# A hybrid decoder trunk on one core: the feed-forward layer in two phases, with seven products per 2x2 block in both

## The chip, the cores and the metric

The kernel runs on one core of one Trainium2 chip. The metric is the device time of one execution in microseconds (us), as the median of three runs.

## What is computed

One step of a decoder layer on 512 new prompt positions (with 16 learned positions ahead of them) and 32 sampled positions, all float32, with a model width of 2048. Attention, a short convolution and a matrix memory are merged by an output projection; then comes the feed-forward layer, which is all that this change touches:

```
x = layer_norm(ALPHA * x + h @ w_out, ln1_g, ln1_b)
u = jax.nn.relu(x @ w_up)                       # w_up 2048 x 8192
return layer_norm(ALPHA * x + (u * u) @ w_down, ln2_g, ln2_b)   # w_down 8192 x 2048
```

It works on 544 columns, one for each position that is an output.

## The kernel before, in words

`phase_project`, `phase_mix`, `phase_out` and `phase_ff` follow one another. `phase_ff` (from L1996) is written out by hand for each engine; semaphores alone order the engines against each other.

**Three matmuls per product.** Every float32 operand is split into a high part, rounded to the type fp32r, and a low part, the difference. ScalarE writes the high part of a weight piece (`high`, L2271), VectorE subtracts it (`low`, L2385), and `third` (L2144 to L2146) makes high x high, high x low and low x high. The parts of the weights lie in rings of three slots, `ring_h` and `ring_l`, each slot 128 x 1024 (8 tiles of 128 x 128). The names `wh`, `big_wh`, `wl`, `big_wl` in a profile are those slots; `big_G` is the PSUM (eight banks); `raw` holds four pieces of raw weights; `base` is a large buffer with `y`, the residual sum in 16 tiles of 128 x 544, and the features `u2` behind it.

**Blocks.** The 8192 features go in 32 blocks of 256 (two tiles of 128). For one block, `up` makes its features from `x`. This product is laid out as 2x2: two feature tiles by two halves of the model width, times two halves of the width by two halves of the columns (272 each). Seven products stand in for eight (Winograd's form of Strassen's scheme): VectorE makes four sums of the weights (`combine`, L2401), the matching sums of `x` were made once, and the results are put together by copies on ScalarE (`copy`, L2311) and additions on VectorE (`accumulate`, L2404). An up block has 7 products x 8 tiles x 3 = 168 matmuls of 128 x 272.

**Down at once.** The features are cut at zero and squared (`relu_square`, L2388), split (`u_high` L2280, `u_low` L2392), and `down` multiplies them with the two row tiles of `w_down` in the ordinary way: 16 output tiles x 2 halves x 2 x 3 = 192 matmuls of 128 x 272. Each output tile is added to `y` by `add` (L2398), so `y` is read and written once per block.

The order is up 1 (plain), down 0, then thirty times up of block b+1 and down of block b (`ff_block` on each engine), then `down_last`, which makes the last down product with the columns as rows and the second layer norm. SyncE (SP) loads the weights: `load_up` (L2090), 512 KB in rows of 512 B, and `load_down` (L2094), 512 KB in rows of 2 KB. GpSimd (POOL) has no work in `phase_ff` until its end.

## Time and profile before

| | us |
|---|---|
| three runs | 2879.74, 2884.47, 2887.08 |
| median | 2884.47 |
| span of the profiled execution | 2886.8 |
| PE busy | 2790.1 (97%) |
| VectorE busy | 1930.4 (67%) |
| ScalarE busy | 889.8 (31%) |
| GpSimd busy | 213.1 (7%) |
| DMA, mean over the span | 196 GB/s |

The profiled execution's own time isn't listed apart; its span, from the first to the last instruction, is 0.3 us under the longest of the three runs. PE is TensorE, PEld its weight loads, DVE VectorE, ACT ScalarE. Matmul records overlap one another in time, so how many of them start in a stretch says more than their durations.

### The profile page before, as it was taken

The page shows a single profiled execution, that of the slowest core. Times are in us where ns is not written, and L with a number is a line of the kernel's source. Part 1 is how long each engine was busy: PE and PEld are TensorE (multiplying, and loading weights), DVE is VectorE, ACT ScalarE, POOL GpSimd, SP SyncE. Part 2 cuts the span into 40 slices and gives each one's busy share as a digit, 9 for nine tenths or more (in the row PEclk, how much of TensorE's full clock was granted, in tenths as well). Part 3 has the DMA queues.
Part 4 walks back from the last instruction along what each step waited for, and adds up shares of the span by engine and source line. Part 5 has one row for each costly group of instructions (what it writes and reads, how often), then busy time and mean ns, then how long its engine had stood idle before and what let it go on. Part 6 is the DMA issues. An engine that isn't in the chain of part 4 may idle for free.

```text
span 2886.8 us, 59355 instructions
## 1 busy us (share of the span) xinstructions
PE 2790.1 (97%) x25779; PEld 2644.1 (92%) x25779; DVE 1930.4 (67%) x2358; ACT 889.8 (31%) x1343; POOL 213.1 (7%) x242
## 2 busy tenths in 40 slices
PE   8999999999999888999999999999999999999997
PEld 8988988888888666999899999999999999999996
DVE  3374555555454586888877777777777777777776
ACT  3221222122122355445523223232232323223232
POOL 3010101101110221111000000000000000000002
PEclk9999999999999899999999999999999999999999
DMA  7889999999999823677323232332323323233232
GB/s 242 307 317 383 412 386 414 409 400 407 396 409 353 282 77 96 172 208 203 92 74 111 67 115 88 88 110 67 117 74 103 103 74 115 66 113 91 86 110 106
DMA packets 379733, 565.95 MB, mean 196 GB/s; under 512 B 22219, under 2 KB 287020, under 8 KB 369058
## 3 DMA queue, kind: packets, MB, share of 16 engines
q1 hardware_dynamic: 302562, 351.68, 37.0%
q0 software_dynamic: 13872, 141.28, 12.1%
q10 hardware_dynamic: 63040, 69.21, 7.0%
q8 instruction: 203, 3.33, 0.5%
q14 instruction: 56, 0.46, 0.0%
HBM read 526.26 MB, written 35.84 MB: 195 GB/s over the span
## 4 chain that ended last, share of the span: by engine, by line
PE 49%; DVE 2%; ACT 0%; DMA 0%; issue 0%; ACTq 0%
PE big_G L2144 16%; PE big_G L2146 16%; PE big_G L2145 16%; DVE ff_mv L2551 0%; DVE ff_out L2556 0%; DVE wl L2385 0%; DMA raw<-in_w_down 0%; PE big_G L2236 0%; DVE base L2401 0%; ACT ff_out L2361 0%; DVE ff_stats L2538 0%; DVE ff_out L2593 0%; ACT wh L2271 0%; DVE base L2398 0%; PE big_G L2232 0%
## 5 line engine op out<-in xcount | busy, mean ns | idle before, releaser
L2398 DVE SCALAR_TENSOR_TENSOR base<-big_G,base 128x544 f32<-128x544 f32 x496 | 358.3, 722 | 230.8 <-PE big_G L2146 230.6
L469 PE MATMUL prj_G<-prj_xh,prj_wh 128*128 128x280 f32 (+1 forms) x1696 | 501.8, 296 | 5.2 <-ACT prj_stage L609 3.3
L471 PE MATMUL prj_G<-prj_xh,prj_wl 128*128 128x280 f32 (+1 forms) x1696 | 496.2, 293 | 0.0
L470 PE MATMUL prj_G<-prj_xl,prj_wh 128*128 128x280 f32 (+1 forms) x1696 | 495.2, 292 | 0.0
L724 DVE STREAM_TRANSPOSE prj_kT<-base 128x4096 f32<-128x4096 f32 x64 | 284.5, 4445 | 263.4 <-PE prj_S L502 260.4
L2271 ACT ACTIVATE wh<-raw 128x1024 fp32r<-128x1024 f32 x227 | 239.4, 1059 | 652.9 <-PE big_G L2146 534.9
L2144 PE MATMUL big_G<-ff_uh,wh 128*128 128x272 f32 x1328 | 382.2, 288 | 1.9 <-DVE base L2398 1.9
L2145 PE MATMUL big_G<-ff_ul,wh 128*128 128x272 f32 x1328 | 383.4, 289 | 0.0
L2146 PE MATMUL big_G<-ff_uh,wl 128*128 128x272 f32 x1328 | 383.4, 289 | 0.0
L469 PEld LDWEIGHTS prj_G<-prj_xh,prj_wh 128*128 128x128 f32 x1696 | 322.4, 190 | 30.0 <-issue 29.3
L2385 DVE TENSOR_TENSOR wl<-raw,wh 128x1024 fp32r<-128x1024 f32 x227 | 277.1, 1221 | 82.0 <-ACT wh L2271 82.0
L471 PEld LDWEIGHTS prj_G<-prj_xh,prj_wl 128*128 128x128 f32 x1696 | 322.4, 190 | 0.0
L470 PEld LDWEIGHTS prj_G<-prj_xl,prj_wh 128*128 128x128 f32 x1696 | 322.2, 190 | 0.0
L2144 PEld LDWEIGHTS big_G<-ff_uh,wh 128*128 128x128 f32 x1328 | 249.4, 188 | 2.4 <-DVE base L2398 2.3
L707 DVE TENSOR_TENSOR prj_wl<-prj_raw,prj_wh 128x1024 fp32r<-128x1024 f32 x106 | 127.1, 1210 | 184.6 <-ACT prj_wh L579 182.9
L2145 PEld LDWEIGHTS big_G<-ff_ul,wh 128*128 128x128 f32 x1328 | 250.3, 188 | 0.0
L2146 PEld LDWEIGHTS big_G<-ff_uh,wl 128*128 128x128 f32 x1328 | 249.7, 188 | 0.0
L2271 ACT ACTIVATE big_wh<-raw 128x1024 fp32r<-128x1024 f32 x113 | 119.6, 1059 | 325.9 <-PE big_G L2146 260.7
L579 ACT ACTIVATE prj_wh<-prj_raw 128x1024 fp32r<-128x1024 f32 x106 | 111.4, 1057 | 339.1 <-DMA prj_raw<-in_w_in 266.5
L2144 PE MATMUL big_G<-big_xh,wh 128*128 128x272 f32 x688 | 201.2, 292 | 1.7 <-ACT base L2274 1.7
L2146 PE MATMUL big_G<-big_xh,wl 128*128 128x272 f32 x688 | 199.2, 289 | 0.0
L2145 PE MATMUL big_G<-big_xl,wh 128*128 128x272 f32 x688 | 197.8, 288 | 0.0
(463 smaller groups left out, 6239.2 us busy)
## 6 DMA issues: line engine op xcount, KB each, us to landing
prj_v_nat<-in_cache_v SPq DMA_DIRECT2D x242, 512.0 KB, 8.4
raw<-in_w_up SPq DMA_DIRECT2D x128, 512.0 KB, 4.5
raw<-in_w_down SPq DMA_DIRECT2D x128, 512.0 KB, 4.5
prj_raw<-in_w_in ACTq DMA_DIRECT2D x103, 512.0 KB
raw<-in_w_out SPq DMA_DIRECT2D x60, 512.0 KB, 4.7
prj_scratch<-prj_stage ACTq DMA_DIRECT2D x53, 280.0 KB, 9.8
out_xr<-x_scratch SPq DMA_DIRECT2D x32, 272.0 KB, 5.3
base<-in_cache_v SPq DMA_DIRECT2D x14, 512.0 KB, 7.9
```

Of the source, the lines that this page charges most:

```text
L469: mm(out, w_hi[:, k, m], xh[:, k0 + k, cols], start=(first and k == 0), stop=False)
L470: mm(out, w_hi[:, k, m], xl[:, k0 + k, cols], start=False, stop=False)
L471: last = mm(out, w_lo[:, k, m], xh[:, k0 + k, cols], start=False, stop=(end and k == nk - 1))
L579: A(wh[n % WH][:, :, :], raw[n % RAW][:, :, :], ACT.Copy).then_inc(hi_done, 1)
L707: V.tensor_tensor(wl[n % WH][:, :, :], raw[n % RAW][:, :, :], wh[n % WH][:, :, :].bitcast(F32), ALU.subtract).then_inc(lo_done, 1)
L724: V.transpose(flat(kT[:, :, :, :, :].rearrange("p r h b i -> p r (h b i)")), flat(k_nat[k % 2][:, :, :]))\
L2144: mm(out, w_hi, x_hi, start=start, stop=False)
L2145: mm(out, w_hi, x_lo, start=False, stop=False)
L2146: return mm(out, w_lo, x_hi, start=False, stop=stop)
L2271: A(ring_h[slot % RING], Q[q], ACT.Copy).then_inc(hi_done, 1)
L2385: V.tensor_tensor(ring_l[slot % RING], Q[q], ring_h[slot % RING].bitcast(F32), ALU.subtract).then_inc(lo_done, 1)
L2398: V.scalar_tensor_tensor(out, G[2 + t % 2][:, :, 0:HALF_M], 1.0 / ALPHA, out, ALU.mult, ALU.add).then_inc(y_done, 1)
```

## The change

The feed-forward layer no longer interleaves up and down products.

Phase one (`for g in range(NUP)`) makes the thirty up blocks 2 to 31, as seven products each. ScalarE now cuts and squares the features (`square`, two instructions of 128 x 1088). For blocks 1 to 30, GpSimd makes four sums of the block's quarters (`made_sum`), so that seven combinations of 128 x 272 lie side by side; ScalarE and VectorE split all seven at once (128 x 1904), and SP spills both parts to DRAM (`u_scratch`). They pass through the room of `y`, which is written to DRAM first (`y_scratch`) and read back at the end of the phase. Blocks 0 and 31 keep their old treatment.

Phase two (`for v in range(NVISIT)`) makes the down products of blocks 1 to 30. Six blocks form a chunk; five chunks by eight pairs of output tiles make 40 visits. A visit is a 2x2 product again, of two tile rows per block by two output tiles, with seven products of 6 tiles x 3 = 126 matmuls of 128 x 272. The combinations of a chunk stand in a window of 20 slots of 128 x 1632 (835,584 bytes each; 14 for a chunk, 6 for the beginning of the next), which takes the room that the split `x` had in phase one. Weight pieces are now 128 x 768 (393,216 bytes), in rows of 512 B, and five of them fit in `raw`.

In both phases one set of four PSUM banks belongs to even groups and one to odd ones, and some products are added onto a bank that already holds one (`onto`). A few semaphores of `phase_project` are cleared and freed, to have enough of them.

Cut to what is spoken of below (the old `ff_block` of each engine stands in the listing above):

```diff
+CH = 6
+NBLK = DFF // (2 * P)
+NUP = NBLK - 2
+NCHK = NUP // CH
+NPAIR = KT // 2
...
+            def fill_window(chunk, n, j):
+                at = 2 * COMBOS * chunk + 2 * n + j
+                slot = AT_SLOT[at % NSLOTS]
+                if at < NSLOTS:
+                    before = BEFORE[at][1]
+                    if before == 7:
+                        sp.wait_ge(combo_lo, NUP)
+                        sp.wait_ge(up_done, product_at(NUP - 1, 2))
+                    else:
+                        sp.wait_ge(up_done, product_at(NUP - 1, before))
+                else:
+                    was, m = divmod(at - NSLOTS, 2 * COMBOS)
+                    sp.wait_ge(up_done, product_at(NUP + NPAIR * was + NPAIR - 1, m // 2))
+                sp.dma_start(window[:, slot, :, :].bitcast(F32), dram["u_scratch"][chunk, j, PLACE[n]]).then_inc(win_in[n], 16)
...
+            for g in range(NUP - 1):
+                sp.wait_ge(lo_done, base_of(g) + 5)
+                load_role(g + 1, 0)
+                sp.wait_ge(sum_done, sums_of(g) + 4)
+                load_role(g + 1, 3)
+                sp.wait_ge(lo_done, base_of(g) + 6)
+                load_role(g + 1, 2)
+                sp.wait_ge(lo_done, base_of(g) + 7)
+                load_role(g + 1, 1)
+                spill(g + 1)
+            g = NUP - 1
+            refill_y(0)
+            for m in range(3):
+                fill_window(0, m // 2, m % 2)
+            sp.wait_ge(lo_done, base_of(g) + 5)
+            load_role(g + 1, 0)
+            for m in range(3, 5):
+                fill_window(0, m // 2, m % 2)
+            sp.wait_ge(lo_done, base_of(g) + 6)
+            load_role(g + 1, 2)
+            sp.wait_ge(lo_done, base_of(g) + 7)
+            load_role(g + 1, 1)
+            load_role(g + 1, 3)
+            for m in range(5, 8):
+                fill_window(0, m // 2, m % 2)
+            spill(g + 1)
+            for m in range(8, 14):
+                fill_window(0, m // 2, m % 2)
+            refill_y(1)
...
+                    for j in range(2):
+                        fill_window(chunk + 1, 3, j)
+                    for j in range(2):
+                        fill_window(chunk + 1, 4, j)
+                    load_next(g, 1)
+                    for j in range(2):
+                        fill_window(chunk + 1, 5, j)
+                    load_next(g, 2)
+                    for j in range(2):
+                        fill_window(chunk + 1, 6, j)
+                    load_next(g, 3)
...
+                    elif wide and n in (3, 5, 6):
+                        pe.wait_ge(copied, 4 + 4 * g + {3: 1, 5: 3, 6: 4}[n])
+                    elif n in (3, 5, 6):
+                        pe.wait_ge(y_done, y_adds(v) + {3: 1, 5: 4, 6: 5}[n])
...
+            def square(b):
+                ac.wait_ge(added, 3 * (b - 1))
+                A(whole_u(b), whole_u(b), ACT.Relu).then_inc(positive, 1)
+                ac.wait_ge(positive, b - 1)
+                A(whole_u(b), whole_u(b), ACT.Square).then_inc(relu_done, 1)
+            def combos_high(b):
+                i = half_of(b)
+                ac.wait_ge(sums_made, 4 * b)
+                if b <= 2:
+                    ac.wait_ge(y_out, 16)
+                else:
+                    ac.wait_ge(spilled[i], 32 * ((b - 1) // 2))
+                A(split[i][0].bitcast(F32R), combos(b), ACT.Copy).then_inc(combo_hi, 1)
+            for n in range(3):
+                high_of(0, n)
+            for g in range(NUP):
+                b, banks = block_of(g), banks_of(g)
+                high_of(g, 3)
+                if b > 2:
+                    ac.wait_ge(combo_lo, b - 2)
+                copy(block_u(b, 0, 0), banks[0], g, 0)
+                high_of(g, 4)
+                if g > 0:
+                    square(b - 1)
+                high_of(g, 5)
+                copy(block_u(b, 1, 0), banks[3], g, 2)
+                copy(block_u(b, 0, 1), banks[0], g, 3)
+                high_of(g, 6)
+                combos_high(b - 1)
+                copy(block_u(b, 1, 1), banks[2], g, 4)
+                for n in range(3):
+                    next_high(g, n)
...
+            def third_and_second(g):
+                low_of(g, 2)
+                dv.wait_ge(*weights_in(g, 2))
+                combine(weights_of(g, 2), weights_of(g, 0), weights_of(g, 2), ALU.subtract)
+                dv.wait_ge(sum_done, sums_of(g) + 1)
+                dv.wait_ge(lo_done, base_of(g) + 3)
+                combine(weights_of(g, 3), weights_of(g, 3), weights_of(g, 2), ALU.subtract)
+            def first_sum(g):
+                dv.wait_ge(sum_done, sums_of(g) + 2)
+                combine(weights_of(g, 0), weights_of(g, 0), weights_of(g, 3), ALU.add)
+            def fourth_sum(g):
+                combine(weights_of(g, 1), weights_of(g, 1), weights_of(g, 3), ALU.subtract)
...
+            def last_add(g):
+                dv.wait_ge(up_done, product_at(g, 6))
+                dv.wait_ge(copied, 4 + 4 * g + 3)
+                accumulate(block_u(block_of(g), 0, 1), banks_of(g)[2])
+            for g in range(NUP):
+                b, banks = block_of(g), banks_of(g)
+                if g > 0:
+                    last_add(g - 1)
+                third_and_second(g)
+                low_of(g, 3)
+                dv.wait_ge(up_done, product_at(g, 1))
+                dv.wait_ge(copied, 4 + 4 * g + 1)
+                accumulate(block_u(b, 0, 0), banks[1])
+                first_sum(g)
+                low_of(g, 4)
+                fourth_sum(g)
+                low_of(g, 5)
+                low_of(g, 6)
+                dv.wait_ge(combo_hi, b - 1)
+                V.tensor_tensor(split[half_of(b - 1)][1].bitcast(F32R), combos(b - 1), split[half_of(b - 1)][0], ALU.subtract).then_inc(combo_lo, 1)
+                next_low(g, 0)
+                dv.wait_ge(up_done, product_at(g, 5))
+                dv.wait_ge(copied, 4 + 4 * g + 4)
+                accumulate(second_tile(b), twice(banks[0]))
+                next_low(g, 1)
...
+                third_and_second(g)
+                if v < NPAIR:
+                    dv.wait_ge(y_in[0 if p < 3 else 1], 16)
+                dv.wait_ge(up_done, product_at(g, 0))
+                to_y(y[:, left, HALVES[0]], banks[0])
+                low_of(g, 3)
+                dv.wait_ge(up_done, product_at(g, 1))
+                dv.wait_ge(y_done, y_adds(v) + 1)
+                to_y(y[:, left, HALVES[0]], banks[1])
+                first_sum(g)
+                dv.wait_ge(up_done, product_at(g, 2))
+                to_y(y[:, right, HALVES[0]], banks[3])
+                low_of(g, 4)
+                fourth_sum(g)
+                dv.wait_ge(up_done, product_at(g, 3))
+                to_y(y[:, left, HALVES[1]], banks[0])
+                low_of(g, 5)
+                low_of(g, 6)
+                dv.wait_ge(up_done, product_at(g, 4))
+                to_y(y[:, right, HALVES[1]], banks[2])
+                if v == NVISIT - NPAIR + 1:
+                    dv.wait_ge(combo_hi, LAST_BLK)
+                    V.tensor_tensor(ul_end, u2_end, uh_end.bitcast(F32), ALU.subtract).then_inc(combo_lo, 1)
+                next_low(g, 0)
+                dv.wait_ge(up_done, product_at(g, 5))
+                dv.wait_ge(y_done, y_adds(v) + 5)
+                to_y(two(y[:, right, :]), twice(banks[0]))
+                next_low(g, 1)
...
+            for b in range(1, NUP + 1):
+                po.wait_ge(relu_done, b + 1)
+                if b == 1:
+                    po.wait_ge(y_out, 16)
+                elif b > 2:
+                    po.wait_ge(combo_lo, b - 2)
+                made_sum(sum_of(b, "T3"), block_u(b, 1, 1), block_u(b, 0, 1), ALU.subtract)
+                made_sum(sum_of(b, "T1"), block_u(b, 0, 1), block_u(b, 0, 0), ALU.subtract)
+                po.wait_ge(sums_made, 4 * b - 3)
+                made_sum(sum_of(b, "T2"), sum_of(b, "T3"), block_u(b, 0, 0), ALU.add)
+                po.wait_ge(sums_made, 4 * b - 1)
+                made_sum(sum_of(b, "T4"), block_u(b, 1, 0), sum_of(b, "T2"), ALU.subtract)
```

**ScalarE, one block.** Before, from the features' split to the next block's first down weights (in names, `base<-big_G` is a copy of a result, 128x1024 a weight piece):

```order
L2280 ACTIVATE ff_uh<-base 128x1088 [waits ff_down_ps,ff_relu_done]
L2271 ACTIVATE wh<-raw 128x1024 [waits ff_sum_done,ff_up_done]
L2311 ACTIVATE base<-big_G 128x272 [waits ff_up_done,ff_low_done]
L2271 ACTIVATE wh<-raw 128x1024 [waits ff_sum_done,ff_up_done]
L2271 ACTIVATE big_wh<-raw 128x1024 [waits ff_up_done]
L2311 ACTIVATE base<-big_G 128x272 [waits ff_up_done]
L2271 ACTIVATE wh<-raw 128x1024 [waits ff_sum_done,ff_up_done]
L2311 ACTIVATE base<-big_G 128x272 [waits ff_up_done]
L2271 ACTIVATE wh<-raw 128x1024 [waits ff_up_done,ff_raw_full0]
L2271 ACTIVATE big_wh<-raw 128x1024 [waits ff_up_done,ff_raw_full2]
L2271 ACTIVATE wh<-raw 128x1024 [waits ff_up_done,ff_raw_full1]
```

After, group g of phase one. The names with prj_ are semaphores of `phase_project` whose numbers were given out anew: `prj_v_last1` is `up_done`, `prj_v_last0` is `lo_done`, `prj_att_in` is `hi_done`; `ff_made` is one of the two buffers of features:

```order
L2494 ACTIVATE wh<-raw 128x1024 [waits prj_v_last1,ff_sum_done]
L2540 ACTIVATE ff_made_20539<-big_G 128x272 [waits prj_v_last1,ff_combo_lo]
L2494 ACTIVATE big_wh<-raw 128x1024 [waits prj_v_last1,ff_sum_done]
L2553 ACTIVATE base<-base 128x1088 [waits ff_added]
L2555 ACTIVATE base<-base 128x1088 [waits ff_positive]
L2494 ACTIVATE wh<-raw 128x1024 [waits prj_v_last1,ff_sum_done]
L2540 ACTIVATE ff_made_20539<-big_G 128x272 [waits prj_v_last1] x2
L2494 ACTIVATE wh<-raw 128x1024 [waits prj_v_last1,ff_sum_done]
L2565 ACTIVATE base<-base 128x1904 [waits prj_aT_ps,ff_sums_made]
L2540 ACTIVATE ff_made_20539<-big_G 128x272 [waits prj_v_last1]
L2494 ACTIVATE big_wh<-raw 128x1024 [waits prj_v_last1,prj_small_in]
L2494 ACTIVATE wh<-raw 128x1024 [waits prj_v_last1,prj_pages_in]
L2494 ACTIVATE wh<-raw 128x1024 [waits prj_v_last1,prj_kt_done]
```

The last copy of a result now stands behind the split of the seven combinations, which waits for GpSimd (`ff_sums_made`); relu and square stand between the weight pieces of products 4 and 5.

**SP, end of phase one.** From the first part of `y` to the first weight piece of the second visit:

```order
L2244 DMA base<-y_scratch 128x6x544 [waits prj_aT_ps,ff_y_out]
L2237 DMA ff_window<-u_scratch 128x1632 [waits prj_v_last1] x3
L2211 DMA raw<-in_w_down 128x6x128 [waits prj_v_last0]
L2237 DMA ff_window<-u_scratch 128x1632 [waits prj_v_last1] x2
L2211 DMA raw<-in_w_down 128x6x128 [waits prj_v_last0] x2
L2211 DMA raw<-in_w_down 128x6x128
L2237 DMA ff_window<-u_scratch 128x1632 [waits prj_v_last1] x3
L2220 DMA u_scratch<-base 128x7x272 [waits ff_combo_lo]
L2220 DMA u_scratch<-base 128x7x272
L2237 DMA ff_window<-u_scratch 128x1632 [waits prj_v_last1,ff_combo_lo] x2
L2237 DMA ff_window<-u_scratch 128x1632 [waits prj_v_last1] x4
L2244 DMA base<-y_scratch 128x10x544 [waits prj_aT_done,ff_y_out]
L2211 DMA raw<-in_w_down 128x6x128 [waits ff_sum_done]
```

Fourteen fills, the last spill and both parts of `y` stand on this queue among the weights of the first visit and ahead of the first piece of the second.

**SP, last visit of a chunk.** From a fill for the next chunk in the visit before it:

```order
L2237 DMA ff_window<-u_scratch 128x1632 [waits prj_v_last1]
L2211 DMA raw<-in_w_down 128x6x128 [waits prj_v_last0]
L2237 DMA ff_window<-u_scratch 128x1632 [waits prj_v_last1] x4
L2211 DMA raw<-in_w_down 128x6x128 [waits prj_v_last0]
L2237 DMA ff_window<-u_scratch 128x1632 [waits prj_v_last1] x2
L2211 DMA raw<-in_w_down 128x6x128 [waits ff_sum_done]
L2237 DMA ff_window<-u_scratch 128x1632 [waits prj_v_last1] x2
```

Eight fills stand between the weight pieces that the next visit needs; all other visits have one or none.

## Rows read from the trace of the kernel before

**Rows 1.** The page: busy time of the engines and the granted clock in 40 slices.
```profile
PE 2790.1 (97%) x25779; PEld 2644.1 (92%) x25779; DVE 1930.4 (67%) x2358; ACT 889.8 (31%) x1343; POOL 213.1 (7%) x242
...
PE   8999999999999888999999999999999999999997
...
PEclk9999999999999899999999999999999999999999
```

**Rows 2.** The page: the chain of work that ended last.
```profile
PE 49%; DVE 2%; ACT 0%; DMA 0%; issue 0%; ACTq 0%
PE big_G L2144 16%; PE big_G L2146 16%; PE big_G L2145 16%; DVE ff_mv L2551 0%; DVE ff_out L2556 0%; DVE wl L2385 0%; DMA raw<-in_w_down 0%; PE big_G L2236 0%; DVE base L2401 0%; ACT ff_out L2361 0%; DVE ff_stats L2538 0%; DVE ff_out L2593 0%; ACT wh L2271 0%; DVE base L2398 0%; PE big_G L2232 0%
```

**Rows 3.** Busy time by stretch; columns as in its first line.
```profile
core 0: us, PE busy (x) PEld busy (x) DVE busy (x) ACT busy (x) POOL busy (x), PEclk, DMA share, GB/s
...
1900.00:2000.00 100.00, 100.00 (x793) 99.71 (x792) 74.14 (x87) 28.72 (x32) 0.00 (x0) 1.00 0.33 95
2000.00:2100.00 100.00, 100.00 (x793) 99.71 (x792) 74.07 (x87) 27.80 (x31) 0.00 (x0) 1.00 0.29 85
```

**Rows 4.** Waits of PE from 1409 to 2831 us: total, times, longest.
```profile
PE big_G L2144 <- DVE base L2398: 5.0, 4, 2.0
PE big_G L2144 <- ACT base L2274: 1.7, 1, 1.7
```

**Rows 5.** Groups by line and form, VectorE, 1409 to 2830 us: busy, mean ns.
```profile
L2398 DVE SCALAR_TENSOR_TENSOR base<-big_G,base 128x544 f32<-128x544 f32 x495 | 357.6, 722 | 230.1 <-PE big_G L2146 229.8
L2385 DVE TENSOR_TENSOR wl<-raw,wh 128x1024 fp32r<-128x1024 f32 x226 | 275.9, 1221 | 82.0 <-ACT wh L2271 82.0
L2401 DVE TENSOR_TENSOR raw<-raw 128x1024 f32<-128x1024 f32 x120 | 146.4, 1220 | 1.0
...
L2404 DVE TENSOR_TENSOR base<-base,big_G 128x272 f32<-128x272 f32 x120 | 52.1, 434 | 1.4
...
L2392 DVE TENSOR_TENSOR ff_ul<-base,ff_uh 128x1088 fp32r<-128x1088 f32 x31 | 39.9, 1286 | 0.5 <-ACT ff_uh L2280 0.5
```

**Rows 6.** The same for ScalarE.
```profile
L2271 ACT ACTIVATE wh<-raw 128x1024 fp32r<-128x1024 f32 x226 | 238.3, 1059 | 647.9 <-PE big_G L2146 529.9 <-DVE raw L2401 98.9 <-DMA raw<-in_w_down 18.9
...
L2280 ACT ACTIVATE ff_uh<-base 128x1088 fp32r<-128x1088 f32 x31 | 34.0, 1097 | 0.0
L2311 ACT ACTIVATE base<-big_G 128x272 f32<-128x272 f32 x90 | 34.0, 378 | 0.0
```

**Rows 7.** Timeline of VectorE in one block: start, duration, instruction, idle before.
```profile
2012.60 1.28 DVE L2392 TENSOR_TENSOR ff_ul<-base,ff_uh 128x1088 fp32r<-128x1088 f32 x1
2013.81 2.48 DVE L2401 TENSOR_TENSOR raw<-raw 128x1024 f32<-128x1024 f32 x2
2017.47 1.22 DVE L2385 TENSOR_TENSOR big_wl<-raw,big_wh 128x1024 fp32r<-128x1024 f32 x1 [1.19 <-ACT big_wh L2271]
2018.61 1.22 DVE L2401 TENSOR_TENSOR raw<-raw 128x1024 f32<-128x1024 f32 x1
2021.02 1.23 DVE L2385 TENSOR_TENSOR wl<-raw,wh 128x1024 fp32r<-128x1024 f32 x1 [1.19 <-ACT wh L2271]
```

**Rows 8.** Timeline where GpSimd and VectorE meet, both reading SBUF.
```profile
1355.99 1.22 DVE L1871 TENSOR_TENSOR big_wl<-raw,big_wh 128x1024 fp32r<-128x1024 f32 x1
1356.15 1.69 POOL L1698 TENSOR_TENSOR out_total<-out_total,base 128x272 f32<-128x272 f32 x1 [6.30 <-DVE base L1889]
1357.13 1.80 DVE L1871 TENSOR_TENSOR out_fourth_l<-raw,out_fourth_h 128x1024 fp32r<-128x1024 f32 x1
```

**Rows 9.** GpSimd line 1698: duration ns minimum, median, maximum.
```profile
L1698 POOL TENSOR_TENSOR out_total<-out_total,base x28: 767/962/1688, 1186.6 to 1374.7; 128x272 f32<-128x272 f32 x28
```

**Rows 10.** DMA traffic: GB/s in 40 slices of 2028 to 2044 us.
```profile
GB/s 36 82 236 266 225 312 399 394 404 344 344 348 326 293 293 288 293 265 92 0 59 83 202 305 334 286 42 41 0 0 0 0 0 0 0 56 77 184 307 348
...
raw<-in_w_up SPq DMA_DIRECT2D x4, 512.0 KB, 4.7
```

**Rows 11.** Busy time by stretch, in the cache stage; last column GB/s.
```profile
600.00:700.00 100.00, 98.12 (x1300) 87.77 (x1300) 53.50 (x30) 22.03 (x39) 11.22 (x8) 1.00 1.02 401
```

**Rows 12.** Busy time by stretch around a gap of PE.
```profile
190.00:194.00 4.00, 4.00 (x61) 3.84 (x64) 2.60 (x3) 2.54 (x8) 0.94 (x1) 1.00 0.79 277
194.00:198.00 4.00, 0.94 (x36) 0.68 (x27) 3.79 (x8) 0.00 (x0) 0.00 (x0) 1.00 0.94 378
198.00:202.00 4.00, 3.09 (x18) 3.10 (x19) 4.00 (x2) 1.54 (x2) 0.00 (x0) 0.75 0.63 237
202.00:206.00 4.00, 4.00 (x28) 4.00 (x27) 2.31 (x2) 0.00 (x0) 1.65 (x1) 0.82 0.22 45
```

563 lines of the change are left out of this document (322 added, 241 removed).

## The prediction

> **What bounds the kernel now.** I read the page first. TensorE is busy for 97% of the span and its clock is full nearly everywhere [rows 1]. The chain that ended last runs through three lines of `phase_ff`, the three matmuls of a product, for 48% of the span [rows 2]. Matmul records overlap, so I count starts: a stretch of 100 us in the feed-forward holds 793 matmuls, which makes 100 / 793 = 0.126 us for one of 128 x 272, with PE never idle, VectorE busy 74% and ScalarE 28% [rows 3]. In the whole layer PE waits 6.7 us [rows 4]. So this layer is worth its number of matmuls, and fewer of them are a gain as long as nothing else becomes the pace. The rest of the argument is about that.
>
> **What goes.** Before, the thirty down blocks have 30 x 192 = 5760 matmuls. Now 40 visits have 126 each, 5040. The up products stay at 30 x 168, and blocks 0 and 31 are as they were. 720 matmuls x 0.126 us = **-91 us**. A group of phase one takes 168 x 0.126 = 21.2 us of PE at the least, a visit 15.9 us.
>
> **Phase one.** The old block lasted 45.4 us (360 matmuls), and the work around the up products could spread under the down products. Now it must fit into 21.2 us. VectorE has per group eleven operations of 128 x 1024 at 1.14 from start to start [rows 7], three additions (two at 0.43, one of 544 columns at about 0.7 [rows 5]) and the low part of the seven combinations. The last is 128 x 1904, which no row shows. The step from 272 to 1088 columns costs 1.286 - 0.434 us for 816 columns, about 1.04 ns a column [rows 5], so it takes 1.29 + 816 x 0.00104 = 2.1 us. That is 16.2 of 21.2 us, so the sum fits. The order doesn't. Follow what must come one after the other, from `square` in one group to `square` in the next:
> - relu and square of 128 x 1088 on ScalarE, 2 x 1.10 [rows 6]: 2.2
> - GpSimd's four sums. One takes 0.77 alone [rows 9]. Where VectorE reads two operands of SBUF at the same time, the record grows to 1.69, since GpSimd starts when VectorE's instruction is over, and VectorE's next one takes 1.80 instead of 1.22 [rows 8]. Low parts 5 and 6 are then on VectorE, so I take two sums of each kind: 4.9
> - the high part of 128 x 1904, by ScalarE's step of (1.097 - 0.378) / 816 = 0.88 ns a column [rows 6]: 1.8
> - its low part: 2.1
> - on VectorE, in program order, next weights 0, second tile, next weights 1, last addition, weights 2, two sums of weights: five at 1.14 (the last, on its predecessor's result, 1.26 [rows 7]), 0.64 and 0.36: 6.8
> - high part 3, low part 3, an addition, a sum, high part 4: two trips to ScalarE of 1.2 [rows 7], then 1.14, 0.36 and 1.22: 5.1
>
> Together 22.9, with the remaining hand-overs 23.0 us. It is longer than PE's 21.2, so the group takes 23.0. PE will be seen to wait before product 7, whose bank is cleared by ScalarE's last copy, and this copy is queued behind the high part of the combinations. 30 x 1.8 = **+54 us**. Bounds: zero stall if the sums never meet VectorE (the loop is then 21.1), and 30 x 3.7 = +111 if all four do (6.8 in place of 4.9).
>
> The Trainium skill (SBUF — State Buffer, Who interferes with whom) says that a VectorE instruction with two SBUF inputs and a GpSimd instruction that reads SBUF hold the shared port for their whole length, and the other blocks. The trace agrees (1.69 and 1.80 above). By the rule alone, with VectorE always there first, the upper bound would be the forecast.
>
> **Between the phases.** All goes through SP's queue, in order. Rates: 512 KB pieces in rows of 512 B move at about 290 GB/s in a burst [rows 10], pieces with long rows at 401 [rows 11], so a fill is 0.836 MB / 401 = 2.1 us and a weight piece 0.393 MB / 290 = 1.4 us. Spills and `y` have rows of 1.1 and 2.2 KB; I take 350 and 400 GB/s for them, between these. From the end of the last but one spill there are queued: `y` part one 4.2, fourteen fills 29, five weight pieces 6.8 (the fifth is the second visit's first), the last spill 5.6, `y` part two 7.0: 52.7 us. That spill is done some 8.5 us into the last up group, so the piece lands at about 8.5 + 52.7 + 1.2 = 62.4 and is split by 64.2, where PE alone would want it at 23.0 + 15.9 = 39. So 25 us of waiting in the first visit and before the second, and about 2 for the clock: **+27 us**. The bounds are +12 (all at 400 GB/s or more) and +45.
>
> On the clock: a gap of some 3 us of PE was followed by 8 us at 0.75 and 0.82 [rows 12], which is 1.0 + 0.7 = 1.7 us lost. I add this to each wait of over 3 us.
>
> **Chunk changes.** In the last visit of a chunk, eight fills stand among the next visit's pieces. From product 1's end (2.3 us, and 1.3 until data flow) the queue has 8 x 2.1 + 3 x 1.4 = 21 us, so role 3, which product 3 of the next visit needs, lands at about 25.8 and is split (0.83 and 0.95 by the rates above) by 27.6. PE alone wants it at 15.9 + 4.5 = 20.4. 7.2 + 1.7 of clock = 8.9, four times: **+35 us**, bounds +16 and +56. In other visits a fill and four pieces are 7.7 of 15.9 us and hidden. The Trainium skill (DMA: Bandwidth & Descriptors, Specifications) gives 512 B as the size from which the full rate is reached. The rows differ (290 against 401 GB/s); by the rule the change of a chunk would cost 4 x 1.2 = 5 us less.
>
> **Visits otherwise.** VectorE has eleven operations of 128 x 768 (0.95, by the step above; 0.88 from start to start), six additions of 0.36 and one of 0.64, 12.5 of 15.9 us. The additions to `y` are one round per chunk instead of per block, 358 us of VectorE before [rows 5], but that cost nothing, being hidden. The tightest place is weights 4: product 2's addition, a sum, a trip to ScalarE and the low part end about 0.3 us before PE wants them. I take 0 and bound it by +0.6 a visit, 24 us. The first group waits for the copy of `y` to DRAM (4.5 MB, about 11 us, and the sums behind it): **+4 us**, bounds 0 and 10. The semaphore clearing and the end of the kernel: 0; the last products keep their form, and their loads are behind waits that end in the last visit.
>
> **Sum** against the profiled span: 2886.8 - 91 + 54 + 27 + 35 + 4 = 2915.8. The median of the runs lies 2.3 us under that span, so I forecast **2914 us**, 1.0% slower. The saving is real, but the work around it is late by more.
>
> **Rivals.**
> - *PE stays the pace in phase one.* GpSimd's sums fall into VectorE's waits (after low part 6 it has nothing to do until the combinations come), the loop closes in 21.2 us. For it: the loop is over by only 8%, and VectorE's sum is 76%. Against it: lows 5 and 6 lie where GpSimd starts. 2914 - 54 = 2860. With the queues also at their better bounds 2860 - 15 - 19 = 2826.
> - *All four sums collide.* 30 x 3.7 instead of 30 x 1.8: 2914 + 57 = 2971. This is what the rule on the shared port gives at its worst. Against it: VectorE has no work for most of that time.
> - *VectorE paces the visits.* 2914 + 24 = 2938. For it: 0.3 us of slack in a chain of eight operations.
> - *Some of each,* with a sum within 0.3% of before. 0.3%, 8.7 us, is about what a measurement here can tell from no change.
> - *The change doesn't do what it says.* The order of PE's queue has exactly 720 matmuls fewer; I give it nothing.
>
> **How the numbers follow.** My forecast (2890 to 2935) 0.49; visits paced by VectorE 0.12; all sums collide 0.07; these are slower: 0.68. PE stays the pace 0.20, faster. Within 0.3%: 0.12. The range is to hold 8 in 10: below, it takes in the first rival, and above, the third and a part of the second: 2855 to 2950.
>
> **What would show it.** Right, if a group of phase one takes about 23 us, with PE waiting 1 to 2 us for a copy of ScalarE's thirty times; if GpSimd's sums have records of 0.8 and 1.7 us side by side; if there are about 25 us of waiting around the first visit, for DMA; and four waits of 6 to 8 us at the third product of a chunk's first visit. Wrong in the main term, if the groups take 21.2 us, or if the visits take more than 16 us in a row.

## The result, and the profile after

The changed kernel takes **2947.2 us** (median of 4 runs, 2934.1 to 2965.0) against 2885.0 before (2879.7 to 2887.1): ratio 1.022, 95% interval 1.019 to 1.025. The forecast was 2914, range 2855 to 2950. The sign was right, the time lies just inside the range, and the change (+62 us) is twice the forecast one (+29). The profiled execution took 2945.5 us, its span is 2943.5.

The page of the changed kernel, to be read against [rows 1] and [rows 2]:

```profile
PE 2730.8 (93%) x25059; PEld 2566.0 (87%) x25059; DVE 1954.3 (66%) x2358; ACT 1086.4 (37%) x1593; POOL 357.2 (12%) x362
...
PE   8999999999998988999999999999969898989897
...
PEclk9999999999999999999999999999989999999998
...
DVE 16%; PE 15%; DMA 8%; ACT 7%; issue 3%; POOL 3%; SPq 0%; ACTq 0%; POOLq 0%
```

PE has its 720 matmuls fewer, and its share fell from 97% to 93%. The chain no longer rests on PE but passes from engine to engine. Waits of PE in three stretches, phase one, between the phases, and the visits after the first (total, times, longest), against 6.7 us in the whole layer before [rows 4]:

```profile
PE big_G L2356 <- ACT ff_made L2540: 19.8, 15, 2.2
PE big_G L2356 <- ACT base L2540: 17.7, 14, 1.3
```
```profile
PE big_G L2356 <- DVE wl L2646: 11.7, 2, 7.7
PE big_G L2356 <- DMA ff_window<-u_scratch: 9.5, 3, 7.0
```
```profile
PE big_G L2356 <- DVE wl L2646: 35.3, 21, 8.1
PE big_G L2356 <- DVE big_wl L2646: 12.3, 13, 7.2
```

In phase one it is the forecast wait, for ScalarE's last copy (L2540), once a group. Of the visits the page does not tell what made VectorE's low halves late; ScalarE's waits in the same stretch do:

```profile
ACT wh L2494 <- DMA raw<-in_w_down: 82.4, 24, 9.8
...
ACT big_wh L2494 <- DMA raw<-in_w_down: 35.3, 12, 9.8
```

ScalarE is held for pieces of `w_down` 36 times, so by far not at the four chunk changes alone: also in ordinary visits, where no such wait was forecast. One of them in ScalarE's timeline:

```profile
2512.05 0.85 ACT L2494 ACTIVATE wh<-raw 128x768 fp32r<-128x768 f32 x1 [1.41 <-PE big_G L2358]
2516.55 0.84 ACT L2494 ACTIVATE big_wh<-raw 128x768 fp32r<-128x768 f32 x1 [3.65 <-DMA raw<-in_w_down]
2520.28 0.85 ACT L2494 ACTIVATE wh<-raw 128x768 fp32r<-128x768 f32 x1 [2.89 <-DVE raw L2658]
```

The 3.65 us before 2516.55 are for the third product's piece. SyncE issues it last of the four, after low half 7.

Dated in the trace, the parts are these. I take a visit's length from one wide addition to `y` (L2784, 128x544) to the next, and a group's from one high part of the combinations (L2565) to the next.

| part | forecast | measured |
|---|---|---|
| matmuls | -91 | -93 (a visit without a wait is 15.83 us) |
| phase one, 30 groups | +54, loop 23.0 | +53, group 22.89 to 23.04 (the first 23.39) |
| between the phases | +27 | +27 |
| four chunk changes | +35 (8.9 each) | +44 (26.9, 25.6, 28.3, 26.9 in place of 15.83) |
| the 35 other visits | 0, bound +24 | +25 (mean 16.5, up to 18.1, and 21 of them over 16) |
| before, and the tail | +4 | +5 (0.9 and 3.8; the first group's wait of 2.2 is in phase one) |

They come to +61 against +57 between the two spans; the 4 us left were not traced. The old layer's 6.7 us of waits are no part of the difference: they stand before 1475 us, and the changed kernel has the same ones there, 5.0 and 1.7 us.

### The profile page after: what moved, and what is told of

The parts are those of the page before. It is cut to its first block, busy times and chain, and to the rows that moved or that the text cites. A ratio compares the mean times of both kernels' runs of the same rounds, so it can differ in the third digit from the quotient of the medians.

```text
span 2943.5 us, 58876 instructions
## 1 busy us (share of the span) xinstructions
PE 2730.8 (93%) x25059; PEld 2566.0 (87%) x25059; DVE 1954.3 (66%) x2358; ACT 1086.4 (37%) x1593; POOL 357.2 (12%) x362
## 4 chain that ended last, share of the span: by engine, by line
DVE 16%; PE 15%; DMA 8%; ACT 7%; issue 3%; POOL 3%; SPq 0%; ACTq 0%; POOLq 0%
DMA raw<-in_w_down 7%; DVE raw L2658 6%; PE big_G L2356 5%; PE big_G L2358 5%; PE big_G L2357 5%; DVE wl L2646 4%; ACT wh L2494 3%; DVE big_wl L2646 2%; ACT big_wh L2494 2%; POOL ff_made L2901 1%; POOL base L2901 1%; ACT base L2565 1%; DVE base L2784 1%; DVE base L2775 1%; DMA u_scratch<-base 1%
## 5 line engine op out<-in xcount | busy, mean ns | idle before, releaser
L2494 ACT ACTIVATE wh<-raw 128x768 fp32r<-128x768 f32 (+1 forms) x333 | 311.0, 938 | 515.3 <-DVE raw L2658 297.7
L2646 DVE TENSOR_TENSOR wl<-raw,wh 128x768 fp32r<-128x768 f32 (+1 forms) x333 | 376.1, 1135 | 184.2 <-ACT wh L2494 184.2
L2356 PE MATMUL big_G<-ff_window,wh 128*128 128x272 f32 x1116 | 330.9, 297 | 54.2 <-DVE wl L2646 47.0
L2358 PE MATMUL big_G<-ff_window,wl 128*128 128x272 f32 x1116 | 325.8, 292 | 0.0
L2357 PE MATMUL big_G<-ff_window,wh 128*128 128x272 f32 x1116 | 325.6, 292 | 0.0
L2658 DVE TENSOR_TENSOR raw<-raw 128x768 f32<-128x768 f32 (+1 forms) x280 | 298.8, 1067 | 2.4
L2356 PEld LDWEIGHTS big_G<-ff_window,wh 128*128 128x128 f32 x1116 | 215.7, 193 | 61.3 <-DVE wl L2646 53.3
L2494 ACT ACTIVATE big_wh<-raw 128x768 fp32r<-128x768 f32 (+1 forms) x167 | 156.5, 937 | 237.4 <-DVE raw L2658 149.5
L2646 DVE TENSOR_TENSOR big_wl<-raw,big_wh 128x768 fp32r<-128x768 f32 (+1 forms) x167 | 189.1, 1132 | 79.6 <-ACT big_wh L2494 79.5
L2356 PE MATMUL big_G<-big_xh,wh 128*128 128x272 f32 x688 | 200.6, 292 | 27.0 <-ACT base L2540 12.7
L2357 PEld LDWEIGHTS big_G<-ff_window,wh 128*128 128x128 f32 x1116 | 215.4, 193 | 0.0
L2358 PEld LDWEIGHTS big_G<-ff_window,wl 128*128 128x128 f32 x1116 | 214.9, 193 | 0.0
## 6 DMA issues: line engine op xcount, KB each, us to landing
prj_raw<-in_w_in ACTq DMA_DIRECT2D x103, 512.0 KB, 16.2
```

Source lines behind the costliest of these rows:

```text
L2356: mm(out, w_hi, x_hi, start=start, stop=False, skip_group_check=onto)
L2357: mm(out, w_hi, x_lo, start=False, stop=False, skip_group_check=onto)
L2358: return mm(out, w_lo, x_hi, start=False, stop=stop, skip_group_check=onto)
L2494: A(ring(ring_h, n, wide), src, ACT.Copy).then_inc(hi_done, 1)
L2646: V.tensor_tensor(ring(ring_l, n, wide), src, ring(ring_h, n, wide).bitcast(F32), ALU.subtract).then_inc(lo_done, 1)
L2658: V.tensor_tensor(out, in0, in1, op).then_inc(sum_done, 1)
```

## The experiments

All times are medians with the kernel before on the same chip (2885.1, 2889.0, 2885.2 and 2885.5 in the four sessions); ratios are to that kernel. 1.022 is the changed kernel. The sessions are experiments 1, 4, 5 and 6; then 2, 3, 8 and 9; then 7, 10 and 11; then 12. Two experiments of different sessions are better compared by their ratios, or by a stretch of their traces, than by their medians.

Some words used below. High half and low half n are ScalarE's and VectorE's parts of the weights for product n of a group, from 1 to 7. The code counts them from 0: `low_of(g, 4)` makes low half 5, which the expectations of experiments 3 and 9 call low half 4. A group's raw weights come as four pieces, which the code calls roles: role 0 is wanted first by product 1, role 1 by product 2, role 3 by product 3, and role 2 by VectorE's first sum, right behind low half 3, and later by product 6.

**1. The square one place earlier.** In `scalar`'s list, `square(b - 1)` stands ahead of high half 4 instead of behind high half 5:

```diff
+                if g > 0:
+                    square(b - 1)
                 high_of(g, 3)
...
                 high_of(g, 4)
-                if g > 0:
-                    square(b - 1)
```

> Relu and square of block b-1 stand on ScalarE ahead of the high part of product 4's weights, where the engine is idle for about 3 us, instead of behind that of product 5's. Theory (phase one is paced by the chain square, sums, split, weights): the chain is cut, since the sums no longer wait for the weights of their own group, and the period falls from 22.9 us to about 21.3, 30 x 1.6 = 48 us less, 2947 - 48 = 2899. Rival (VectorE with its delays behind GpSimd is the pace, or the place of the last copy alone): the period stays over 22.5, less than 12 us gained.

Measured: 2933.5 us, 1.018 (1.014 to 1.022); the theory's 2899 was missed. The wait for the copy is gone, but behind the first a group still takes 22.1 to 23.8 us, 22.6 on the mean, where PE alone would take 21.2. That is 9 us less in phase one; the medians differ by 14. Waits of PE and of ScalarE, 1500 to 2100 us:

```profile
PE big_G L2356 <- DVE wl L2646: 19.1, 26, 1.0
PE big_G L2356 <- DVE big_wl L2646: 7.0, 9, 0.8
```
```profile
ACT wh L2494 <- DMA raw<-in_w_up: 85.8, 25, 5.7
...
ACT big_wh L2494 <- DMA raw<-in_w_up: 38.4, 9, 4.4
```

So there is a second loop behind the first, through the load of the piece of role 1. The chain over one group (start, length, what) shows it whole:

```profile
1701.97 6.28 DMA raw<-in_w_up
...
1708.27 1.07 ACT big_wh L2494
...
1717.26 1.37 DVE raw L2658
...
1718.66 1.07 ACT big_wh L2494
...
1719.75 1.22 DVE big_wl L2646
1720.97 1.14 DVE raw L2658
1722.11 2.36 DVE wl L2646 x2
1724.49 6.28 DMA raw<-in_w_up
```

From load to load 22.5 us, 6.3 of them from the issue of a piece to its landing. No term of my sum had this loop.

**2. The four sums left out** (what is spilled for blocks 3 to 30 is stale). This asks from the other side whether the first loop was the only one:

```diff
-                G_.tensor_tensor(out, in0, in1, op).then_inc(sums_made, 1)
+                if b > 2:
+                    po.sem_inc(sums_made, 1)
+                else:
+                    G_.tensor_tensor(out, in0, in1, op).then_inc(sums_made, 1)
```

> GpSimd's four sums of the squares are left out for blocks 3 to 30 (the spilled sums are then stale); everything else is the changed kernel's, the late square too. Theory (the loop copies, square, sums, split, low halves, next copies paces phase one at 22.9): the loop loses the 4.97 us of the sums and ends at about 18; the next bound paces, TensorE's 21.2 or the loads that ride on the low halves, so 28 groups fall by 1 to 1.7: 2900 to 2920, and TensorE's wait for 'base L2540' goes from 1.3 to near 0. Rival (the write of the spilled block or VectorE's list of work paces the group, and the sums lie beside it): a group stays at 22.9, 2940 to 2950.

Measured: 2931.7 us, 1.015 (1.013 to 1.017), above the expected 2900 to 2920. The wait for the copy went (1.0 us is left), so the loop through the sums was the pace at 22.9. But 5 us taken from it shorten a group by 0.3 us only, to 22.6, the same as in experiment 1. ScalarE's waits, same stretch:

```profile
ACT wh L2494 <- DMA raw<-in_w_up: 72.9, 17, 6.0
ACT big_wh L2494 <- DVE raw L2658: 60.4, 18, 4.2
ACT big_wh L2494 <- DMA raw<-in_w_up: 28.8, 9, 3.6
```

**3. The fourth sum ahead of low half 5** (`low_of(g, 4)`), with the early square, in phase one:

```diff
                 first_sum(g)
-                low_of(g, 4)
                 fourth_sum(g)
+                low_of(g, 4)
```

> The square one place earlier, as in the run with that edit alone (2933.5 us, one group 22.35 to 23.26), and in phase one VectorE makes the fourth sum ahead of its part of low half 4. Theory (a second loop): with the early square, ScalarE waits 85.8 + 38.4 us for the pieces of w_up in 1500:2100, because the loads of a group's first halves are given to SyncE after the low halves 5 to 7, which stand behind the fourth sum; the loop through the load is as long as the loop through the sums. The sum ahead takes 1.2 us out of both loops: one group near 21.4, little above TensorE's 21.2, the time 2933 - 30 x 1.4 = 2891 (2880 to 2905). Rival (the load's landing alone paces the group, whatever VectorE's order): a group stays at 22.3, 2925 to 2940. Second rival: VectorE's low half 4, one place later, holds TensorE's fifth product: a group of 22.6 or more, 2940 and above.

Measured: 2962.0 us, 1.026 (1.023 to 1.029), a group 23.3 on the mean. My theory of how to shorten this loop fell, and the outcome lies where the second rival put it. Two steps of the chain:

```profile
1706.69 7.69 DMA raw<-in_w_up
...
1729.91 8.52 DMA raw<-in_w_up
```

From the landing to this piece's next issue the loop is indeed shorter (1714.4 to 1729.9, 15.5 us, against 1708.3 to 1724.5, 16.2), but from issue to landing it takes 7.7 and 8.5 us instead of 6.3. SyncE's timeline shows why. Its four issues of a group, in experiment 1 and here:

```profile
1721.00 4.05 SPq L2198 DMA_DIRECT2D raw<-in_w_up  x4
```
```profile
1727.63 4.02 SPq L2198 DMA_DIRECT2D raw<-in_w_up  x4
```

In experiment 1 the piece of role 1, the last of the four, is issued 3.5 us behind the first, here 2.3 us (2.6 on the mean): the three pieces ahead of it left closer together. Counted from the first issue, what follows hardly moves. The third piece lands 8.3 us behind it in experiment 1 and 8.2 here (means over 1500 to 2100 us), and ScalarE gets the piece of role 1 after 9.8 and 10.3 us (medians). So what counts for this loop is when the first of the four leaves. It waits for low half 5, and this is just what the sum now stands in front of: from the landing at 1714.4 to the next first issue at 1727.6 are 13.2 us, against 12.7 (1708.3 to 1721.0) in experiment 1. The edit took work away from the last issue and put it ahead of the first. PE's waits for low halves rose from 26 to 40 us.

**4. Pieces ahead of the fills at a chunk change.** SyncE's list:

```diff
-                    for j in range(2):
-                        fill_window(chunk + 1, 4, j)
                     load_next(g, 1)
-                    for j in range(2):
-                        fill_window(chunk + 1, 5, j)
                     load_next(g, 2)
-                    for j in range(2):
-                        fill_window(chunk + 1, 6, j)
                     load_next(g, 3)
+                    for n in (4, 5, 6):
+                        for j in range(2):
+                            fill_window(chunk + 1, n, j)
```

> In the last visit of a chunk, SP issues one pair of fills, then the three weight pieces for the next visit, then the other six fills. Theory (the pieces stand behind the fills in the queue): the four changes, now 26.9 us from one visit's wide addition to the next against 15.9 in an undisturbed one, fall to 18 or less, 4 x 9 = 36 us less, 2911. Rival (the fills themselves come too late, whatever their order, or the queue's rate is the limit): the wait moves to products 5 to 7 for the window and less than 12 us are gained.

Measured: 2906.0 us, 1.007 (1.005 to 1.010). The changes take 18.5 to 18.8 us instead of 25.6 to 28.3: 33 of the 41 us gained are these. No wait of PE over 2 us is left in the visits behind the first. That the fills in front of the pieces cost the time is shown.

**5. `y`'s second part read back later**, in the first visit's list instead of ahead of it (`refill_y(1)` moved from before the loop of visits to the end of its first round).

> The second part of y (2.8 MB) is read back behind the weight pieces of the second visit instead of ahead of them. Theory (the queue is served in order and is what the second visit waits for): its 7 us go from the first passage between the phases, 29 us over PE's own time falls to about 22, 2940. Rival (the window fills, not the pieces, are late): no change, 2947.

Measured: 2931.6 us, 1.016 (1.011 to 1.021). The first wide addition to `y` is at 2184.1 instead of 2195.3 us, but 4 of these 11 us are there before the edit comes into play: the last high part of the combinations is at 2143.7 instead of 2147.8. The other 7 us are the edit's, as expected. PE's waits around the second visit, 2180 to 2200 us in the changed kernel and 2180 to 2215 here:

```profile
PE big_G L2356 <- DVE wl L2646: 7.7, 1, 7.7
```
```profile
PE big_G L2357 <- DVE wl L2647: 2.4, 4, 0.6
```

The medians differ by 16 us, with runs of 2919.6 to 2943.2 here.

**6. The order of two pieces.** `IN_ORDER = (0, 1, 2, 3)`, and the piece for the third product (role 3) takes the place of role 2's in each round of SyncE. With the place goes the wait: role 3 is now issued behind low half 6, role 2 behind low half 7.

```diff
                     load_next(g, 1)
-                    load_next(g, 2)
                     load_next(g, 3)
+                    load_next(g, 2)
```

> The order of the five places in raw is changed, so that the piece for product 3 takes the place that is free after low part 6 instead of 7, about 0.9 us earlier, and the piece that is only needed by the first sum takes the late one. Theory (ordinary visits lose 0.6 us on average because product 3's piece is issued last and lands late): 36 visits x 0.4 = 15 us less, 2932, with fewer waits of ScalarE for w_down. Rival (VectorE's order is late in the visits, or the late landings hit every piece alike): less than 5 us either way.

Measured: 2922.9 us, 1.013 (1.011 to 1.017). Ordinary visits are 15.80 to 15.85 nearly everywhere, the changes stay at 26.3 to 27.7: 24 us, the ordinary visits' whole loss, where 15 were expected.

**7. The piece for the third product not loaded at all**, from the third visit on (the product works on what lies in the buffer):

```diff
+                if g > NUP + 1 and role in (3,):
+                    sp.sem_inc(five_full[m % 5], 16)
+                    return
```

> From the third visit on, the piece of w_down for the third product (role 3) is not loaded; its semaphore is counted up when SyncE comes to it, and the product works on what lies in the buffer. Nothing else is changed, the order of the other pieces included. Theory (ordinary visits lose 0.7 us each, and chunk changes part of their 11, because this piece is the last to be given out and lands too late for the high half of the third product): the ordinary visits go to 15.83 +- 0.1, as when the pieces change places (2922.9), the chunk changes from 26.9 to 22 or less since the last piece behind the window's fills is gone: 2895 to 2918. Rival (another piece or VectorE's order holds the visits, and the changed order only moved it): visits stay at 16.3 to 16.6 on the mean, 2930 to 2947.

Measured: 2897.8 us, 1.004 (1.001 to 1.006). The ordinary visits are 15.80 to 15.85, the changes 20.2 to 22.5, phase one still 22.91. Waits of PE after the first visit, which were 35.3 and 12.3:

```profile
PE big_G L2359 <- DVE wl L2649: 10.9, 6, 4.1
...
PE big_G L2359 <- DVE big_wl L2649: 2.9, 3, 2.5
```

With VectorE's list and every other piece as they were, the visits run at PE's pace. So it was this piece, not VectorE's order. It also makes 24 of the 44 us that the chunk changes lose; 20 us are left without it.

**8. Edits 1, 4, 5 and 6 together.**

> The four edits together: square one place earlier, pieces ahead of the window's fills at a chunk change, the read back of y's second part later, the piece for product 3 issued ahead of the one for product 7. If the four places are separate in time, their gains add: -14 for phase one, -37 for the four chunk changes, -14 between the phases, -24 for the other visits: 2947 - 89 = 2858 (2850 to 2872), 1% below the kernel before. Rival (the gains are one gain, the time in which the DMA queue is late, counted several times): 2900 or above.

Measured: 2869.4 us, 0.993 (0.991 to 0.995): faster than both kernels. By the medians the four gains sum to 14 + 41 + 16 + 24 = 95 us, of which 78 were had (84 by the ratios). What each edit changed in its own stretch of its trace is 9 (groups), 33 (changes), 7 (`y`) and 24 (visits), 73 us. The visits are as foreseen (15.8, changes 18.7 to 19.7). A group of phase one is 22.8 us long, a little more than the 22.6 of experiment 1, some 4 us in all.

**9. The same with the fourth sum ahead.**

> The four edits and the fourth sum ahead of low half 4 in phase one. Theory as for these parts: phase one at 21.4 a group instead of 22.4, 30 us less than the four edits alone, 2828 (2815 to 2845), 2% below the kernel before. Rival (VectorE or the landing of the loads paces phase one): equal to the four edits, about 2858.

Measured: 2891.6 us, 1.000 (0.999 to 1.002), a miss of 64 us: the sum ahead costs some 21 us here and 23 in experiment 3, by the ratios.

**10. The spilled block's writes later.** With the four edits, what makes the load of role 1 take 6 to 8 us? Either the two writes of 952 KB issued behind it take its share, or the three pieces in front of it do:

```diff
                 load_role(g + 1, 1)
+                sp.wait_ge(lo_done, base_of(g + 1) + 2)
                 spill(g + 1)
```

> The four edits (2869.4), and in phase one SyncE waits for low half 2 of the next group before it issues the two writes of a spilled block (952 KB each), so they leave after the piece of role 1 has landed. Theory A (the writes share the DMA queue with the piece in flight and stretch its 6 to 7.7 us from issue to landing): it lands some 1.5 to 2 us earlier, a group comes down from 22.6 to 21.4 to 21.8, 2835 to 2850. Theory B (the piece is late because three other pieces of 512 KB stand in front of it in the queue, 2.1 MB at some 295 GB/s being 7.1 us, and the writes stand behind it): no change, 2862 to 2878.

Measured: 2878.1 us, 0.997 (0.995 to 0.999); a group 22.7, as without the edit (22.8), so no gain in phase one, as theory B says. The 9 us more lie behind it: from the last high part of the combinations to the first wide addition to `y` it is 48.8 us instead of 42.2. There the last but one spill, which stands ahead of the reads of `y` and of the window on the queue, leaves later, and PE waits 7.2 us before the first product of the first visit, where it waited 0.4.

**11. Role 1 ahead of role 2 in phase one.**

```diff
-                sp.wait_ge(lo_done, base_of(g) + 6)
-                load_role(g + 1, 2)
                 sp.wait_ge(lo_done, base_of(g) + 7)
                 load_role(g + 1, 1)
+                load_role(g + 1, 2)
                 spill(g + 1)
```

> The four edits (2869.4), and in phase one the piece of role 1, which the second product needs, is issued before the piece of role 2, which the sixth needs. Theory B (queue position): role 1 has 512 KB less in front of it, which at 295 GB/s is 1.8 us, and leaves SyncE up to 1.0 us sooner; a group comes down from 22.6 to TensorE's 21.2 to 21.6, 29 times: 2832 to 2850, 1.5% below the kernel before. Theory A (the writes behind it are what slows it): role 1 gains little, since it is issued after low half 7 either way, 2860 to 2878. Rival: role 2 is now late for the sixth product, or VectorE's list paces the group, 2865 or more.

Measured: **2832.6 us, 0.982 (0.980 to 0.985)**, 37 us less than experiment 8 for two lines exchanged (31 by the ratios), and 1.8% below the kernel before. In the traces phase one is 37 us shorter: 623 us in place of 660 from the first high part of the combinations to the last. Waits of PE in phase one, 1500 to 2100 us, which were 26 us in experiment 1 and 28 in experiment 8:

```profile
PE big_G L2351 <- DVE wl L2641: 3.0, 6, 0.8
PE big_G L2351 <- DVE big_wl L2641: 1.9, 3, 0.8
```

The chain from 1700 to 1760 us, by line, and the page's line of busy times:

```profile
by line: PE big_G L2351 26.8%; PE big_G L2353 26.3%; PE big_G L2352 26.2%; DVE raw L2653 6.3%; issue 3.7%; ACT big_wh L2489 3.6%; DVE wl L2641 2.4%; DVE big_wl L2641 2.1%; ACT wh L2489 1.8%; DVE ff_made L2656 0.7%; DVE base L2656 0.7%
```
```profile
PE 2710.8 (96%) x25059; PEld 2558.9 (90%) x25059; DVE 1940.2 (68%) x2358; ACT 1093.5 (39%) x1593; POOL 374.5 (13%) x362
```

A group averages 21.5 us and PE is the pace of phase one again, with the sums of GpSimd and the spills all in. This settles the second loop: it is one piece's position in one queue. The Trainium skill (DMA: Bandwidth & Descriptors, Queues, rings and completion order) says that each DMA engine takes the descriptors of a queue in their order; experiments 10 and 11 agree, nothing a group for what stands behind the piece and 1.3 us a group for what stands ahead.

**12. The same exchange alone**, on the changed kernel with its late square. Are these two loops, or one cause seen twice?

> The exchange of role 1 and role 2 in phase one's issues, alone, on the changed kernel with its late square. Theory (two loops, one behind the other; the longer one sets the group): the loop through the sums and the copies, 22.90 us, does not contain this load, so a group stays at 22.9 and PE's wait for ScalarE's copy (16.5 + 16.4 us in 1500 to 2100) stays: 2940 to 2950, ratio 1.019 to 1.025. Rival (there is only one cause, the late load, and the wait for the copy is its consequence): a group falls to 21.5 as with the four edits, about 2905 to 2915.

Measured: 2942.0 us, 1.018 (1.013 to 1.023). The groups are 22.88 to 22.90 us long and PE waits as before:

```profile
PE big_G L2355 <- ACT base L2539: 16.3, 13, 1.3
PE big_G L2355 <- ACT ff_made L2539: 16.3, 13, 1.3
```

ScalarE's waits for `w_up` fell (21.6 + 13.0 us in the changed kernel, 10.9 + 5.5 here), and no group got shorter. The exchange that is worth 37 us behind the early square is worth nothing measurable in front of it: two loops, and the longer one sets the group.

## Why the prediction was right in sign and short by half

**Matmuls: right.** A visit in which PE waits for nothing takes 15.83 us; 126 x 0.126 was 15.9.

**Phase one: right, with its loop.** The sum of steps gave 23.0 us, and nearly all groups of the trace have 22.89 to 22.96. The two steps that no row showed, and the one that was bounded, came out as estimated. Groups of ScalarE and VectorE by form, and GpSimd's timeline:

```profile
L2565 ACT ACTIVATE base<-ff_made 128x1904 fp32r<-128x1904 f32 x15 | 26.9, 1793 | 39.1 <-POOL ff_made L2901 39.1
```
```profile
L2775 DVE TENSOR_TENSOR base<-ff_made,base 128x1904 fp32r<-128x1904 f32 x15 | 32.1, 2143 | 37.5 <-ACT base L2565 37.5
```
```profile
1730.51 4.97 POOL L2901 TENSOR_TENSOR ff_made<-ff_made 128x272 f32<-128x272 f32 x4 [18.07 <-ACT ff_made L2555]
```

Forecast 1.8, 2.1 and 4.9. Taking the sums away removed PE's wait for the copy, so the loop is shown, not only argued. What the analysis lacked is the second loop 0.3 us behind it (experiments 1, 2, 11 and 12). For the forecast this cost nothing; for the rival "PE stays the pace in phase one" it means that its condition, sums that fit in VectorE's waits, would not have sufficed: without any sums the kernel is still at 2932, not 2860.

**Between the phases: right.** +27 for +27, and 7 of it are the second part of `y`, which may come later (experiment 5). Busy time by stretch; the last columns are the granted clock, DMA share and GB/s:

```profile
core 0: us, PE busy (x) PEld busy (x) DVE busy (x) ACT busy (x) POOL busy (x), PEclk, DMA share, GB/s
1900.00:2000.00 100.00, 94.93 (x741) 93.41 (x740) 76.74 (x68) 51.78 (x60) 19.54 (x16) 1.00 0.60 182
2136.00:2236.00 100.00, 76.62 (x553) 74.88 (x552) 57.37 (x73) 31.68 (x38) 4.88 (x4) 0.90 0.77 265
```

741 matmuls in 100 us of phase one stand against 793 before [rows 3]. In the 100 us around the first visit only 553 start, at a granted clock of 0.90.

**Chunk changes: right mechanism, too small.** "7.2 + 1.7 of clock = 8.9, four times" measured 11.1 each, +44 in place of +35. The four waits stand where they were forecast, at the third product of each chunk's first visit. The first of them (the longest wait in 2300 to 2346 us), and the stretch behind it:

```profile
PE big_G L2356 <- DVE wl L2646: 8.1, 1, 8.1
```
```profile
2324.00:2328.00 4.00, 4.00 (x20) 4.00 (x21) 3.41 (x6) 0.84 (x1) 0.00 (x0) 0.55 0.00 0
```

The others are 7.2, 8.1 and 8.1 us, 7.9 on the mean where 7.2 were reckoned. Shorter waits make 0.5 us a change. The other 2.7 come without a wait, in place of the 1.7 taken for the clock: in the 4 us above the granted clock is 0.55, near the lower of its two levels, and 20 matmuls start where 32 would at 0.126 us. Experiment 4 shows the fills as the cause. Experiment 7 leaves 20 of the 44 us with the third product's piece gone; then PE waits 2.5 to 4.1 us at the fourth product.

**"Visits otherwise ... I take 0": the step that failed.** It measured +25, and with it came the prediction's own sign of being wrong, visits of more than 16 us in a row. Of the 28 us by which the span (2943.5) lies over the forecast one (2915.8), 25 are this term and 9 the chunk changes; the other parts take off 6. I looked for the danger in VectorE's order ("the tightest place is weights 4") and bounded it by +24, nearly the right size for the wrong reason. The pieces were dismissed in one clause, "a fill and four pieces are 7.7 of 15.9 us and hidden". That is a statement on the amount moved. What counts is when the last piece leaves and who wants it first: the third product's piece is issued after low half 7, behind the other three, and is wanted 4.5 us into the next visit. In the ordinary visits it took 3.9 to 6.4 us from issue to landing, and the visit's length follows it. Two such pieces, issued at 2510.1 and at 2528.2 us:

```profile
DMA to landing us min/median/max: 6.4/6.4/6.4
```
```profile
DMA to landing us min/median/max: 3.9/3.9/3.9
```

The visits around them take 18.07 and 15.83 us. In all 28 ordinary visits that could be set against their piece, the length (from SyncE's first issue of one to that of the next) is 15.83 us as long as the piece takes no more than 4.2, and beyond that it is longer by what the piece takes over 4.2, to within 0.03 us. Why one piece takes 3.9 and another 6.4 us stays open. Experiment 6 gives the whole +25 back by exchanging two pieces (role 3 then leaves 0.9 us earlier), experiment 7 by dropping the one. The rival "VectorE paces the visits" (2938) was the nearest to the time, and its mechanism is refuted: VectorE's work is the same in experiment 7.

**The tail: taken as 0, measured +3.8.** One wait for the last four pieces, which stand behind the last visit's low halves:

```profile
PE big_G L2434 <- DMA raw<-in_w_down: 3.9, 1, 3.9
```

It is in every variant (3.8 to 4.5 us) and I tried nothing against it.

**The shared port.** GpSimd's sums in 1500 to 2100 us, those on one of the two buffers; the three numbers are the shortest, median and longest in ns:

```profile
L2901 POOL TENSOR_TENSOR ff_made<-ff_made x55: 758/806/1763, 1501.2 to 2098.5; 128x272 f32<-128x272 f32 x55
```

Of the four sums at 1730.51 two take 0.81 and 0.77 us and two 1.75 and 1.65, 4.97 in all, as two free ones and two colliding ones would (2 x 0.77 + 2 x 1.69 = 4.9), not the 6.8 of all four colliding. Beside the last two, VectorE's low halves took 1.71 us in the chain of the changed kernel instead of the 1.22 of [rows 5], as in [rows 8]. The rule of the Trainium skill (SBUF — State Buffer, Who interferes with whom) agrees with this; its worst case, VectorE always there first (2971), did not come: VectorE starts only two instructions beside the four sums, low halves 6 and 7 (the prediction's low parts 5 and 6), the first of them 0.9 us behind the first sum. The other rule, on rows of 512 B, was worth 5 us and no run separates it.

## What to carry to other kernels

When fewer matmuls shrink a block, every loop that ran in its shade becomes a candidate for the pace. Look for the second one before mending the first: here loops of 22.9 and 22.6 us lay one behind the other, and mending one alone took 0.3 us off a group (experiment 1) or nothing (12), while the second mend on top of the first took off 1.3 (11). A loop passes through DMA as well: buffer free, issue, the pieces ahead in the queue, landing, conversion, product.

For weights streamed through one in-order queue, do not ask whether the bytes fit in the period. Write down for each piece when its buffer is free, what stands ahead of it, when it lands, and when its product wants it; then issue in the order of need. Exchanging two pieces was worth 24 us in one phase and 37 in the other.

## What the runs showed that I had not expected

- A piece of 512 KB, 1.8 us of data at the 290 GB/s of the burst in [rows 10], takes 6.3 to 8.5 us from the end of its wait to its landing when three others were issued just before it. Counted from the first of the four issues it is about 10 us, however they are spaced. Behind it, two writes of 952 KB each do not make a group longer (experiment 10).
- Moving 1.1 us of VectorE's work from ahead of the last issue to ahead of the first (experiment 3) made the kernel nearly 1% slower than experiment 1.
- GpSimd's four sums take 4.97 us in the changed kernel and 5.96 with the early square, for the same work: three of the four then take 1.65 to 1.79 us instead of two.
